# Decay arguments moved from VectorE to ScalarE, and the slots of an SSD group redrawn, in a one-core encoder block

## The reference

```
h  = rms_norm(x);  u = h @ w_in                 # q | k | v | z | x | B | C | dt
A  = dilated window attention of q, k, v        # 16 heads of 128
xbc = silu(depthwise_conv5(x | B | C))
per direction: dt = softplus(dt_raw + bias);  a = -exp(a_log) * dt;  a_cum = cumsum(a) in chunks of 128
    Lmat[l, s] = exp(a_cum[l] - a_cum[s]) for s <= l, else 0
    y = (C B^T * Lmat) (x dt)  +  the part carried over from the other chunk
y  = rms_norm_per_group((y_fwd + y_bwd + xs * d_skip) * silu(z))
x  = x + concat(A, y) @ w_out
x  = x + relu(rms_norm(x) @ w_up)^2 @ w_down
```

## Time and profile before

| | |
|---|---|
| median of three runs | 1587.81 us (1587.65 to 1588.23) |
| the profiled execution, whole | 1587.99 us |
| its span | 1586.3 us |
| TensorE busy | 1533.9 us (97%) |
| VectorE busy | 1016.3 us (64%) |
| ScalarE busy | 727.2 us (46%) |
| windows 1 to 4 together (99.5 to 439.9 us) | 340.4 us |

### The profile page before, as it was taken

How to read it: one execution, slowest core, us unless ns; L and a number is a source line. 1 busy time by engine, 2 the same in 40 slices (tenths; PEclk the granted TensorE clock), 3 DMA queues, 4 the chain that set the end, 5 groups by cost and what they waited for, 6 DMA issues and landing times.

```text
span 1586.3 us, 25891 instructions
## 1 busy us (share of the span) xinstructions
PE 1533.9 (97%) x9501; PEld 1374.6 (87%) x9501; DVE 1016.3 (64%) x1553; ACT 727.2 (46%) x851; POOL 24.2 (2%) x29
## 2 busy tenths in 40 slices
PE   6999999898999999999999999999999999999998
PEld 6999888886788888888889998899988998889987
DVE  5889899999976666565556555455554555545553
ACT  4355555454664544544344443434433444334432
POOL 0000000000101000000000000000000000000000
PEclk9999999999999999999999999999999999999999
DMA  8875556555565666565556655566556665656552
GB/s 255 253 221 175 142 177 169 161 181 175 160 191 174 184 174 185 175 233 175 193 186 179 183 183 196 177 182 178 193 192 177 183 186 191 194 165 183 186 196 95
DMA packets 186338, 291.60 MB, mean 184 GB/s; under 512 B 13533, under 2 KB 67151, under 8 KB 185984
## 3 DMA queue, kind: packets, MB, share of 16 engines
q1 hardware_dynamic: 183748, 285.92, 59.5%
q10 hardware_dynamic: 2492, 4.36, 0.9%
HBM read 288.04 MB, written 5.34 MB: 185 GB/s over the span
## 4 chain that ended last, share of the span: by engine, by line
PE 77%; DVE 14%; issue 5%; DVEq 1%; ACT 1%; DMA 0%; ACTq 0%
PE psum L1142 75%; DVE w_lo L748 3%; DVE mix L774 3%; DVE conv L794 2%; DVE mix L765 2%; DVE cbm L805 1%; DVE xbc L799 0%; DMA x_in<-in_x 0%; PE psum L1241 0%; PE psum L1261 0%; ACT w_hi L463 0%; PE psum L1187 0%; DVE gate_t L812 0%; ACT conv_t L490 0%; DVE conv L790 0%
## 5 line engine op out<-in xcount | busy, mean ns | idle before, releaser
L748 DVE TENSOR_TENSOR w_lo<-raw,w_hi 128x1024 fp32r<-128x1024 f32 x512 | 624.8, 1223 | 457.6 <-ACT w_hi L463 454.0
L463 ACT ACTIVATE w_hi<-raw 128x1024 fp32r<-128x1024 f32 x512 | 540.5, 1057 | 734.9 <-PE psum L1142 732.2
L1142 PE MATMUL psum<-actT_lo,w_hi 128*128 128x256 f32 x1792 | 514.6, 287 | 11.8 <-DVE w_lo L748 11.8
L1142 PE MATMUL psum<-actT_hi,w_hi 128*128 128x256 f32 x1792 | 510.6, 285 | 0.0
L1142 PE MATMUL psum<-actT_hi,w_lo 128*128 128x256 f32 x1792 | 510.5, 285 | 0.0
L1142 PEld LDWEIGHTS psum<-actT_lo,w_hi 128*128 128x128 f32 x1792 | 347.7, 194 | 20.4 <-DVE w_lo L748 13.2
L1142 PEld LDWEIGHTS psum<-actT_hi,w_lo 128*128 128x128 f32 x1792 | 347.6, 194 | 0.2
L1142 PEld LDWEIGHTS psum<-actT_hi,w_hi 128*128 128x128 f32 x1792 | 347.4, 194 | 0.0
L1142 PE MATMUL psum<-w_hi,hid_lo 128*128 128x512 f32 x512 | 199.2, 389 | 0.0
L1142 PE MATMUL psum<-w_lo,hid_hi 128*128 128x512 f32 x512 | 199.2, 389 | 0.0
L1142 PE MATMUL psum<-w_hi,hid_hi 128*128 128x512 f32 x512 | 199.2, 389 | 0.0
(11 more groups left out here) (188 smaller groups left out, 1124.5 us busy)
## 6 DMA issues: line engine op xcount, KB each, us to landing
raw<-in_w_in SPq DMA_DIRECT2D x128, 512.0 KB
raw<-in_w_up SPq DMA_DIRECT2D x128, 512.0 KB
raw<-in_w_down SPq DMA_DIRECT2D x128, 512.0 KB
raw<-in_w_out SPq DMA_DIRECT2D x64, 512.0 KB
raw<-in_w_in SPq DMA_DIRECT2D x64, 256.0 KB
raw<-in_w_in SPq DMA_DIRECT2D x128, 128.0 KB
decay<-decay_rows SPq DMA_DIRECT2D x16, 512.0 KB, 5.2
rel_tiles<-rel_rows ACTq DMA_DIRECT2D x1, 3072.0 KB, 19.5
```

The costliest lines, as they stand in the source:

```text
L463: act.activation(w_hi[j % RING][:, :, :], raw[j][:, :, :], ACT.Copy).then_inc(hi_ready, 1)
L748: tt_(w_lo[i][:, :, :], raw[j][:, :, :], w_hi[i][:, :, :].bitcast(f32), ALU.subtract).then_inc(lo_dve, 1)
L1142: return pe.matmul(o, lhsT, rhs, start=first, stop=last, **kw)
```

## The change

Five edits:

- **Decay arguments.** `decay_args` leaves VectorE and becomes ScalarE work, in k = 5, 6, 8 and 9 (`ARG_SLOTS`). Four of the six blocks of 128 columns are now Relu of (-decay - token number), with a negated copy `tokn` of the token numbers, and are later exponentiated with scale -1; the two others, which need no minimum, are written as exponentials at once. `head_exp` becomes two instructions of 2 x 128 columns in place of one of 768.
- **First slot.** Transposes and C B^T move from the end of k = 1 to the end of k = 0, `mask_cb` and `mix_head` to k = 1 to 4, y to the ends of k = 4 and 6, and the z work to slot 0 of a window.
- **Gate to norm.** The gate and the squares move to k = 7, `sq_lo` stays at k = 8, `group_mean` moves to k = 10, `group_norm` joins `group_low` in k = 11. Logarithm and exponential stay at k = 10.
- **Convolution.** The five taps stand in k = 0, 5, 6, 8 and 9, the tanh and the SiLU in k = 10.
- **Loads.** The decay rows of a window's second group are issued by SyncE in slot 11, not 13.

The core of the diff:

```diff
-CONV_SLOTS = {0: (0, 1), 1: (2,), 6: (3,), 7: (4,)}
+CONV_SLOTS = {0: (0,), 5: (1,), 6: (2,), 8: (3,), 9: (4,)}
+ARG_SLOTS = {5: 0, 6: 1, 8: 2, 9: 3}
...
-                if s == 13 and m is not None:
+                if s == 11 and m is not None:
                     sp.wait_ge(args_ready, 8 * m + 4)
                     load_decay(2 * m + 1)
...
+            def decay_args(G, h):
+                H, w = 4 * G + h, mix[h]
+                act.wait_ge(decay_in, 32 * (G + 1))
+                act.wait_ge(y_done, H + 1)
+                f, b = ds(H, 1), ds(32 + H, 1)
+                for k, d, l, src, col in ((0, 0, 0, 0, f), (2, 0, 1, 1, f), (3, 1, 0, 0, b), (5, 1, 1, 1, b)):
+                    act.activation(w[:, k, :], decay[:, d, h, P * l:P * l + P], ACT.Relu,
+                                   bias=tokn[:, src, col], scale=-1.0)
+                act.activation(w[:, 1, :], decay[:, 0, h, P:2 * P], ACT.Exp, bias=tokp[:, 2, f])
+                act.activation(w[:, 4, :], decay[:, 1, h, 0:P], ACT.Exp, bias=tokp[:, 2, b]).then_inc(args_ready, 1)
+
             def head_exp(H, h):
                 act.wait_ge(args_ready, H + 1)
-                act.activation(mix[h][:, :, :], mix[h][:, :, :], ACT.Exp).then_inc(decays_ready, 1)
+                act.activation(mix[h][:, 0:3:2, :], mix[h][:, 0:3:2, :], ACT.Exp, scale=-1.0)
+                act.activation(mix[h][:, 3:6:2, :], mix[h][:, 3:6:2, :], ACT.Exp, scale=-1.0).then_inc(decays_ready, 1)
...
-                    if k == 2:
+                    if k == 1:
                         act.wait_ge(x_transposed, G + 1)
...
-                    if k == 8:
+                    if k == 7:
                         act.wait_ge(gated, G + 2)
...
-                    if k == 8 and (i == 0 or more):
+                    if k == 10 and (i == 0 or more):
                         conv_tanh_of(G + 1)
+                    if k in ARG_SLOTS and (i == 0 or more):
+                        decay_args(G + 1, ARG_SLOTS[k])
...
-                    if s == 2:
+                    if s == 0:
                         z_tanh_of(m)
...
-                if k == 9:
+                if k == 10:
                     silu(G)
-                if 8 <= k < 12:
-                    decay_args(G, k - 8)
...
-                    if k == 2:
+                    if k == 1:
                         mask_cb(G)
-                    if 2 <= k < 6:
-                        mix_head(G, k - 2)
-                    if k == 8:
+                    if 1 <= k < 5:
+                        mix_head(G, k - 1)
+                    if k == 7:
                         gate_group(G, i, m)
...
-                    if k == 9:
+                    if k == 10:
                         group_mean(G)
-                    if k == 10:
+                    if k == 11:
                         group_norm(G)
-                    if k == 11:
                         group_low(G)
...
-                    if k == 1:
+                    if k == 0:
                         pe.wait_ge(xbc_ready, G + 1)
...
-                    if k in (5, 7):
+                    if k in (4, 6):
                         pe.wait_ge(xtok_ready, G + 1)
-                        pe.wait_ge(mix_ready, 4 * G + k - 3)
+                        pe.wait_ge(mix_ready, 4 * G + k - 2)
```

More of the change, by code:

```diff
@@ L132, in build @@
         tokp = place("tokp", [P, 5, 64])
+        tokn = place("tokn", [P, 2, 64])
         phase = top[0]
@@ L597, in _ @@
                     xbc_copy(1, 1, 0)
-                if s == GROUP_SLOT[1] + 8:
+                if s == GROUP_SLOT[1] + 10:
                     conv_tanh_of(0)
+                if s - GROUP_SLOT[1] in ARG_SLOTS:
+                    act.wait_ge(m1_free, 1)
+                    decay_args(0, ARG_SLOTS[s - GROUP_SLOT[1]])
             def ssd_window(w, m):
@@ L753, in low_ahead @@
                 low(U0 + n, j)
[L756 to L766, removed]
             def mix_head(G, h):
@@ L1020, in dt_tokens @@
                 dve.wait_ge(dt_tok, 1)
+                ts_(tokn[:, :, :].rearrange("p a h -> p (a h)"), M1[:, 0:128], -1.0, None, ALU.mult)
                 dve.tensor_copy(tokp[:, :, :].rearrange("p a h -> p (a h)"), M1[:, 0:320]).then_inc(m1_free, 1)
@@ L1205, in ssd_slot @@
                         ins.then_inc(cb_done, 1)
-                    if k in (5, 7):
+                    if k in (4, 6):
                         pe.wait_ge(xtok_ready, G + 1)
-                        pe.wait_ge(mix_ready, 4 * G + k - 3)
+                        pe.wait_ge(mix_ready, 4 * G + k - 2)
                         for t in range(TT):
-                            for h in (k - 5, k - 4):
+                            for h in (k - 4, k - 3):
                                 ins = mm(M0[64 * (h % 2):64 * (h % 2) + 64, SEQ * (h // 2):SEQ * (h // 2 + 1)],
```

## The result

The changed kernel takes 1597.6 us (median of 4 runs, 1596.3 to 1598.7) against 1587.7 for the kernel before: ratio 1.0058, interval 1.0047 to 1.0070. It is slower, by 9.9 us. Its profiled execution took 1597.19 us, 9.2 more than that of before. The forecast was 1590.2, its range 1580 to 1598.

The account below looks back on a forecast made before the run. VectorE's list, work plus waits, was taken to bound windows 1 to 4. Against 1587.99 us, -4.3 + 0.2 + 5.5 + 0.8 = +2.2 us gave 1590.2 us, range 1580 to 1598.

Parts of the forecast that it names:

- The bound: Windows 1 to 4: they run at the pace of VectorE's list, its work plus its waits.
- The three waits: VectorE waits for ScalarE: 2.3 us behind the gate, 2.9 or 3.8 at the norm, 1.35 at the output.
- The 0.15 for the first chunk of k = 0: Start of a group: VectorE's first chunk waits 0.15 us for its `w_hi`.
- ScalarE's sets: Six argument activations per head on ScalarE: 1.8 us a set, bounds 1.2 and 2.5, hidden behind VectorE's taps.
- the bound of 2.1: ScalarE before the last tap: two sets and two chunks fit up to 2.1 us a set; twice the excess lengthens the path.
- The rival that they are too long: ScalarE's sets cost over 2.1 us; at 2.5, 0.8 us in each of seven distances: 1596; chance 8%.
- The turn of the loop: Ends of windows 1 and 2: a turn costs 0 to 2.6 us, twice; taken as 0.
- the rival of 1595.4: The loop's turn still stalls 2.6 us at the end of windows 1 and 2, +5.2 us; chance 20%.
- First gate: Sum's first term: the first gate follows one chunk and two taps less, -4.3 us.
- First gate to the gate of group 6: Sum's second term: three distances of 43.8 and three of 44.0, 263.4 us against 263.2, +0.2.
- End of the gate of group 6 to the end of window 4: Sum's third term: 52.4 us against 46.9, +5.5; a further 0.8 for TensorE's wait and clock.
- The parts named for it: Slower side, 0.43: 15 of the forecast's 45%, both slow rivals, half of the rest.

Follow-up runs that it names:

- the two edits of ScalarE's queue: Changed kernel, separately: squares listed behind the next rounded chunk, 1588.4 us; logarithm and exponential listed behind the chunk of slot 11, 1587.4 us.
- the later squares: Changed kernel with the gate's two squares on ScalarE listed behind the next slot's rounded chunk: 1588.4 us, ratio 1.0004.
- the short sets: Changed kernel with a head's six argument activations replaced, from group 1 on, by one of 768 columns writing zeros: 1597.2 us, ratio 1.0062.
- the code written out: VectorE's loop over windows 1 to 3 as straight code: 1581.3 us from the kernel before, 1591.3 us from the changed kernel.
- the shifted list: Changed kernel with 136 tiny VectorE instructions more in window 0, ahead of the loop: 1598.9 us, ratio 1.0071.
- the moved work alone: Kernel before, its slots untouched, with only the decay arguments moved to ScalarE and their load earlier: 1589.6 us, ratio 1.0007.

## Why the prediction was right or wrong

- **The bound** was right. VectorE's list, work plus waits, sets windows 1 to 4 in both kernels: the turns, 5.0 and 4.6 us, brought 6.8 and 6.3, and the distances fell by as much as the two edits of ScalarE's queue shortened VectorE's waits (1.6 us, and 1.15). The exception is the later squares in the first two windows, where ScalarE waits for TensorE.
- **The three waits** were right to 0.15 us: 2.31 (2.3 in the walk) behind the gate, 2.93 and 3.84 (2.9 and 3.8) at the norm, 1.41 and 1.50 (1.35) at the output. The 0.15 for the first chunk of k = 0 did not appear. A distance inside a window is 44.0 us for 43.8.
- **ScalarE's sets** were right: 1.75 us (1.8 in the sum), hidden, with a margin of 0.78 us for two, so by these rows they would have fitted up to 2.14 each. That agrees with the bound of 2.1. The rival that they are too long is out by the 1.75 us and by the short sets.
- **The turn of the loop is the step that failed.** I took 0 for it, because 296 instructions are nearer to the short lists than to 398. It costs 2.35 and 2.29 us, 4.6 in all, nine tenths of what it cost before. This was the rival of 1595.4, to which I gave 20%. VectorE's lists of 398 and 296 pay 2.3 to 2.6 us, ScalarE's of 217 shows nothing. As far as these lists tell, the cost is a step between 217 and 296 and no slope, and an interpolation was the wrong tool. By the Trainium skill (Runtime: NRT & Kernel Launch, section Instruction fetch mechanics) a taken branch waits for a fetch when its target is outside the two pages of 256 instructions. The trace agrees in that a fetch stands in each idle piece, and the code written out has neither at that place. The pages themselves it does not show: by the places named for the shifted list (120 to 416, then 256 to 552) the 296 instructions would fit into two pages both times if these are counted from the list's start, and yet they pay.
- **The sum.** First gate: -3.6 us for -4.3. Of the 0.7 us between, 0.36 are a wait for a rounded chunk at 120.71, behind the first of the two taps that precede the gate, and 0.12 are there when the window's first chunk starts (100.94 for 100.82); the rest is in small parts. First gate to the gate of group 6: 269.2 us for 263.4, of which the turns are 4.6 us and the other 1.2 come in small parts, 0.2 in each inner distance and up to 0.3 over the ends. End of the gate of group 6 to the end of window 4: 52.1, with whatever the clock took, for 52.4 + 0.8. So the forecast's +2.2 becomes 2.2 + 0.7 + 5.8 - 1.1 = +7.6, and the chain of waits says the same: TensorE starts its work behind window 5's first transposes at 450.99, before at 443.29, 7.7 us later.

```profile
450.99 2.77 PE psum L1150 x12
```

- **The rest,** 1.5 of the 9.2 us of the two profiled executions, lies in one quarter of the MLP, and such a step is found in the other kernels too (see the last section).
- **The chances.** The sign came out on the side with the largest of the three chances, 0.43. The parts named for it add up to 0.46 (0.15 + 0.20 + 0.08 + half of 0.07), with 0.30 for "same"; the three chances given don't quite follow from them. Had the turn been taken at the 2.3 to 2.6 us of the rows, the forecast would have been 1595.

## What to carry to other kernels

Work that is taken off a full engine counts only as far as nothing on that engine waits behind it: walk its new list item by item beside the list of the engine that feeds it, and look for the items that used to fill a wait. In an engine's queue put what the other engine needs next ahead of what it needs later: two edits of one line each were worth 9 and 10 us here, while the moved work alone changed nothing that can be measured. And the cost of a loop's turn, 2.3 to 2.6 us for both of VectorE's lists here, is better taken over whole from a list of the same order than scaled by its length, or bought off by writing the loop out.

## What was not expected of the hardware

There is a step of 1.5 us in the MLP that differs between executions. TensorE's quarters of 1152 matmuls take 180.7 to 181.0 us or 179.5. The third of the four quarters of before, and the same one of after (the chain of waits):

```profile
1218.70 179.50 PE psum L1142 x1152
```

```profile
1226.45 180.99 PE psum L1150 x1152
```

The stretches at their start (columns as above) show it as TensorE's granted clock, 1.00 against 0.94. In pieces of 2 us the slow one starts at 0.66 and 0.50 (1226.4 to 1230.4) and then has 0.99, where the other has 1.00 from its start; so it begins with some 4 us in which the clock is at the lower of the two levels (1.2 GHz) or comes back from it. Both stand behind the same idle time of TensorE, 2.73 us:

```profile
1218.00:1248.00 30.00, 29.30 (x244) 29.30 (x245) 17.34 (x15) 11.58 (x12) 0.00 (x0) 1.00 0.66 200
```

```profile
1226.00:1256.00 30.00, 29.55 (x234) 29.55 (x235) 15.96 (x15) 11.39 (x11) 0.00 (x0) 0.94 0.65 194
```

In the thirteen profiled executions of this case 6 of 39 such quarters are the short kind, in kernels of every sort. What decides it stays open. Executions of one kernel also differ by more (the later squares by 5.1 us, from 1586.6 to 1591.7), which was not followed up. A difference of 1.5 us between two single executions says nothing.
